# Folding the Newton step of the mLSTM head finish, and reordering the work around it and around the output projection that follows

## What is computed

```python
def _head_norm(x, g):
    xc = x - jnp.mean(x, axis=-1, keepdims=True)
    y = xc * lax.rsqrt(jnp.mean(xc * xc, axis=-1, keepdims=True) + NORM_EPS)
    return y.reshape(x.shape[:2] + (-1,)) * g
...
        hc = num / jnp.maximum(jnp.abs(den), jnp.exp(-m_t))[..., None]
...
    out_d = jax.nn.sigmoid(o_pre) * _head_norm(hm, P['mlstm_gn_g'][j])
    y = jnp.concatenate([out_c, out_d], axis=-1) @ P['c_w_out'][j]
    ...
        x = x + g1 * y
```

## Time and profile before

| | us |
|---|---|
| median of 3 runs (1537.2 to 1539.61) | 1537.5 |
| the profiled execution's own time | 1538.78 |
| its span, first to last instruction | 1537.2 |
| TensorE matmul busy in the span (93%) | 1428.2 |
| VectorE busy (58%) | 892.0 |
| ScalarE busy (33%) | 508.9 |
| GpSimd busy (8%) | 127.5 |

### The profile page before, as it was taken

One profiled execution on the slowest core, in us unless ns is written; L12 is line 12 of the kernel. 1 busy time (PEld: TensorE's weight loads), 2 busy tenths in 40 slices (PEclk: granted clock), 3 DMA queues, 4 the chain that ended last, 5 costly groups with the idle time before them and its releaser, 6 DMA issues.

```text
span 1537.2 us, 28543 instructions
## 1 busy us (share of the span) xinstructions
PE 1428.2 (93%) x11003; PEld 1353.7 (88%) x11003; DVE 892.0 (58%) x1613; ACT 508.9 (33%) x755; POOL 127.5 (8%) x149
## 2 busy tenths in 40 slices
PE   6899999969999999999679999987799999999997
PEld 4789898869999999999669897876699999999997
DVE  4565675578876885587764556664553433333344
ACT  4254345232222221222443334533332212222233
POOL 0000000002211220021000000000001101100100
PEclk9899999989999999999879899988899999999999
DMA  9443343325554554353222213221213223232222
GB/s 327 155 131 117 124 145 113 125 68 170 173 152 138 165 165 137 97 169 101 49 57 56 67 32 91 78 61 32 82 55 93 85 86 87 88 95 83 82 75 80
DMA packets 231853, 164.67 MB, mean 107 GB/s; under 512 B 9990, under 2 KB 218568, under 8 KB 231636
## 3 DMA queue, kind: packets, MB, share of 16 engines
q1 hardware_dynamic: 219716, 120.57, 26.8%
q0 software_dynamic: 11744, 42.75, 8.3%
q10 hardware_dynamic: 304, 0.10, 0.0%
HBM read 159.80 MB, written 3.60 MB: 106 GB/s over the span
## 4 chain that ended last, share of the span: by engine, by line
PE 75%; DVE 11%; ACT 7%; issue 4%; DMA 2%; SPq 0%; DVEq 0%; ACTq 0%; POOLq 0%
PE ring L604 67%; ACT weight_high L415 1%; DVE weight_low L420 1%; PE core_j L532 1%; DMA weight_raw<-in_c_w_in 1%; PE core_k L1317 1%; PE ring L2147 1%; PE ring L2229 1%; PE core_j L482 1%; DVE norm_rstd L614 1%; DVE norm_step L612 1%; PE core_k L1320 0%; DVE norm_step L611 0%; DVE normed_low L700 0%; DVE residual L710 0%
## 5 line engine op out<-in xcount | busy, mean ns | idle before, releaser
L604 PE MATMUL ring<-normed_high,weight_high 128*128 128x272 f32 x2128 | 454.7, 295 | 38.0 <-DVE normed_low L700 24.9
L604 PE MATMUL ring<-normed_high,weight_low 128*128 128x272 f32 x2128 | 446.2, 292 | 0.0
L604 PE MATMUL ring<-normed_low,weight_high 128*128 128x272 f32 x2128 | 445.4, 291 | 0.0
L604 PEld LDWEIGHTS ring<-normed_high,weight_high 128*128 128x128 f32 x2128 | 340.6, 192 | 49.0 <-issue 39.9
L604 PEld LDWEIGHTS ring<-normed_low,weight_high 128*128 128x128 f32 x2128 | 341.0, 192 | 0.0
L604 PEld LDWEIGHTS ring<-normed_high,weight_low 128*128 128x128 f32 x2128 | 338.9, 192 | 0.0
L420 DVE TENSOR_TENSOR weight_low<-weight_raw,weight_high 128x1024 fp32r<-128x1024 f32 x197 | 257.5, 1308 | 71.1 <-ACT weight_high L415 69.6
L415 ACT ACTIVATE weight_high<-weight_raw 128x1024 fp32r<-128x1024 f32 x197 | 206.8, 1050 | 164.7 <-PE ring L604 152.3
L604 PE MATMUL ring<-mixed_high,weight_high 128*128 128x272 f32 x960 | 203.6, 294 | 18.3 <-DVE weight_low L420 7.7
L604 PE MATMUL ring<-mixed_high,weight_low 128*128 128x272 f32 x960 | 200.7, 291 | 0.0
L604 PE MATMUL ring<-mixed_low,weight_high 128*128 128x272 f32 x960 | 199.9, 290 | 0.0
(11 more groups left out here) (403 smaller groups left out, 1166.9 us busy)
## 6 DMA issues: line engine op xcount, KB each, us to landing
weight_raw<-in_w_ffn_in SPq DMA_DIRECT2D x88, 512.0 KB, 3.7
mod_weight<-in_w_mod POOLq DMA_DIRECT2D x48, 512.0 KB, 4.2
mod_weight<-in_w_mod POOLq DMA_DIRECT2D x16, 1024.0 KB, 5.5
weight_raw<-in_w_ffn_out SPq DMA_DIRECT2D x32, 512.0 KB, 3.7
weight_raw<-in_a_w_in SPq DMA_DIRECT2D x24, 512.0 KB, 3.9
weight_raw<-in_c_w_in SPq DMA_DIRECT2D x20, 512.0 KB, 3.9
mixer_area<-in_w_mod SPq DMA_DIRECT2D x8, 1024.0 KB, 8.8
weight_raw<-in_w_ffn_out SPq DMA_DIRECT2D x16, 384.0 KB, 3.2
```

What stands on the lines that cost most here:

```text
L604: last = pe.matmul(PS[p.slot][:, half, 0:HALF], w[n.slot][:, k, :], x[:, k, half * HALF:(half + 1) * HALF], start=(k == 0 and w is WH and ...
```

## The change

The finish of the mLSTM heads is rewritten. With the centred values c, the first guess y of the reciprocal root and the variance v, it computes c (1 + gate) y (y y v - 3), with the gain changed from 0.5 to -0.25, instead of 0.5 c (1 + gate) times a separately refined y. The product c (1 + gate) is made early on VectorE, y y on ScalarE. The copies of the head out of PSUM go from ScalarE to VectorE. ScalarE's table load goes ahead of the weight copy in the loop. VectorE does the attention ahead of the low part of the head before. For the last head the squared floors are summed with the variance by matmuls, and Ln and the product read the sum from PSUM. The last k-tile of the first two output units is issued for both units with the high parts first. At the start of both output projections ScalarE makes the third unit's high weights ahead of the first square; in layer 1 VectorE makes its low weights ahead of the first sum.

```diff
...
         s_fth = sem("ffn_tanh")
+        s_hsq = sem("head_rstd_squared")
         s_area, s_smw, s_wg = sem("area_cleared"), sem("small_weights_in"), sem("decay_weights_in")
...
                 for j in range(2):
-                    if not (end and j) and not (first and j == 0):
+                    if first and j == 0:
+                        hi_of(act, Turn(w, 2))
+                    elif not (end and j) and not first:
                         hi_of(act, Turn(w, j + 1, 2, i))
...
                 for j in range(size):
-                    if not (end and j == size - 1) and not (first and j == 0):
+                    if not (end and j == size - 1) and not first:
                         lo_of(dve, Turn(w, j + 1, size, i))
                     residual_dve(dve, Turn(w, j, size, i), Turn(p, j, size, i), gate, i * size + j)
+                    if first and j == 0:
+                        lo_of(dve, Turn(w, 2))
                     if q is not None:
...
                     pe.wait_ge(s_glo, KD + (k + 1 if k >= HEADS else HEADS))
-                    last = product(pe, n, p, k, KD, (GH, GL))
-                if k == KD - 1:
-                    last.then_inc(s_used, 1)
+                    product(pe, n, p, k, KD, (GH, GL))
...
                 head_var(pe, OSQ, s_osq, h + 2 * HEADS)
+
+            def last_var():
+
+                pe.wait_ge(s_d2, HEADS)
+                pe.matmul(K[:, 0, :], MEAN[:, :], DD[:, 0:TP], start=True, stop=False)
+                pe.matmul(K[:, 1, 0:TS], MEAN[:, :], DD[:, TP:T], start=True, stop=False)
+                pe.wait_ge(s_osq, 3 * HEADS)
+                pe.matmul(K[:, 0, :], MEAN[:, :], OSQ[:, 0:TP], start=False, stop=True)
+                pe.matmul(K[:, 1, 0:TS], MEAN[:, :], OSQ[:, TP:T], start=False, stop=True).then_inc(s_var, 1)
+
+            def last_tile():
+
+                turns = [(Turn(W_OUT1, j), Turn(R_OUT1, j)) for j in range(2)]
+                k = KD - 1
+                pe.wait_ge(s_gah, 2 * KD + DONE0)
+                for n, p in turns:
+                    for w in (WH, WL):
+                        for half in range(2):
+                            pe.matmul(PS[p.slot][:, half, 0:HALF], w[n.slot][:, k, :],
+                                      GH[:, k, half * HALF:(half + 1) * HALF], start=False, stop=False)
+                pe.wait_ge(s_glo, 2 * KD)
+                for n, p in turns:
+                    for half in range(2):
+                        last = pe.matmul(PS[p.slot][:, half, 0:HALF], WH[n.slot][:, k, :],
+                                         GL[:, k, half * HALF:(half + 1) * HALF], start=False, stop=True)
+                    last.then_inc(s_used, 1)
...
             out1(1, range(4, 6))
-            var_of(HEADS - 1)
+            last_var()
             out1(1, range(6, 7))
-            out1(0, range(7, 8))
-            out1(1, range(7, 8))
+            last_tile()
...
-            def head_copies(h):
-                copy_head(act, st, s_nd, h + 2 * HEADS, h + 1)
+            def floors(h):
+                act.wait_ge(s_nd, h + 1)
                 act.wait_ge(s_nv, h + 2 * HEADS)
...
             def rstd(h):
-                act.preload_act_table_set("natural_log_exp_and_others")
-                act.wait_ge(s_nv, h + 2 * HEADS + 1)
-                st.done(act.activation(NR[:, :], NV[:, :], ACT.Ln))
+                if h < HEADS - 1:
+                    act.wait_ge(s_nv, h + 2 * HEADS + 1)
+                    st.done(act.activation(NR[:, :], NV[:, :], ACT.Ln))
+                else:
+                    act.wait_ge(s_var, 3 * HEADS)
+                    st.add(act.activation(NR[:, 0:TP], K[:, 0, :], ACT.Ln))
+                    st.done(act.activation(NR[:, TP:T], K[:, 1, 0:TS], ACT.Ln))
                 act.activation(NR[:, :], NR[:, :], ACT.Exp, scale=-0.5).then_inc(s_hr0, 1)
+                act.wait_ge(s_hr0, h + 2 * HEADS + 1)
+                act.activation(NT[:, :], NR[:, :], ACT.Square).then_inc(s_hsq, 1)
...
                 if h:
-                    head_copies(h - 1)
+                    floors(h - 1)
                 else:
...
                 values(h)
+                if h:
+                    act.preload_act_table_set("natural_log_exp_and_others")
                 hi_of(act, Turn(W_ML, 2 * h + 3))
...
                     gate(h + 1)
-            head_copies(HEADS - 1)
+            floors(HEADS - 1)
             squares(HEADS - 1)
+            act.preload_act_table_set("natural_log_exp_and_others")
             rstd(HEADS - 1)
...
             def floors(h):
+                dve.wait_ge(s_nd, h + 1)
+                st.add(dve.tensor_copy(OT[:, 0:TP], K[:, 0, :]))
+                dve.tensor_copy(OT[:, TP:T], K[:, 1, P:P + TS]).then_inc(s_o, 1)
                 dve.wait_ge(s_dabs, h + 1)
...
+            def gated(h):
+
+                dve.wait_ge(s_oc, h + 2 * HEADS + 1)
+                dve.wait_ge(s_dabs, h + 1)
+                st.add(dve.scalar_tensor_tensor(out=OB, in0=GATES[h % 2], scalar=1.0, in1=OC, op0=ALU.add,
+                                                op1=ALU.mult))
+
             def finish(h):
                 dve.wait_ge(s_var, h + 2 * HEADS + 1)
-                dve.wait_ge(s_d2, h + 1)
-                st.add(dve.tensor_tensor(NV[:, 0:TP], K[:, 0, :], DD[:, 0:TP], ALU.add))
-                dve.tensor_tensor(NV[:, TP:T], K[:, 1, 0:TS], DD[:, TP:T], ALU.add).then_inc(s_nv, 1)
-                dve.wait_ge(s_nv, h + 2 * HEADS + 1)
                 if h < HEADS - 1:
+                    dve.wait_ge(s_d2, h + 1)
+                    st.add(dve.tensor_tensor(NV[:, 0:TP], K[:, 0, :], DD[:, 0:TP], ALU.add))
+                    dve.tensor_tensor(NV[:, TP:T], K[:, 1, 0:TS], DD[:, TP:T], ALU.add).then_inc(s_nv, 1)
+                    dve.wait_ge(s_nv, h + 2 * HEADS + 1)
                     lo_of(dve, Turn(W_ML, 2 * h + 5))
                 dve.wait_ge(s_hr0, h + 2 * HEADS + 1)
-                newton(dve, st, NV[:, :], NR[:, :], NT[:, :])
-                st.done(dve.tensor_tensor(NT[:, :], OC, NR[:, :], ALU.mult))
-                dve.scalar_tensor_tensor(out=OB, in0=GATES[h % 2], scalar=1.0, in1=NT[:, :], op0=ALU.add,
+                st.wait()
+                st.add(dve.tensor_tensor(OB, OB, NR[:, :], ALU.mult))
+                dve.wait_ge(s_hsq, h + 1)
+                if h < HEADS - 1:
+                    st.done(dve.tensor_tensor(NT[:, :], NT[:, :], NV[:, :], ALU.mult))
+                else:
+                    st.add(dve.tensor_tensor(NT[:, 0:TP], NT[:, 0:TP], K[:, 0, :], ALU.mult))
+                    st.done(dve.tensor_tensor(NT[:, TP:T], NT[:, TP:T], K[:, 1, 0:TS], ALU.mult))
+                dve.scalar_tensor_tensor(out=OB, in0=NT[:, :], scalar=-3.0, in1=OB, op0=ALU.add,
                                          op1=ALU.mult).then_inc(s_ob, 1)
+
+            def low(h):
+                dve.wait_ge(s_ob, h + 2 * HEADS + 1)
                 dve.wait_ge(s_gah, h + KD + HEADS + DONE0 + 1)
...
                 norm_column(h)
+                if h:
+                    gated(h - 1)
                 keys(h)
...
                 attention(h)
+                if h:
+                    low(h - 1)
                 if h < HEADS - 1:
...
             floors(HEADS - 1)
+            gated(HEADS - 1)
             finish(HEADS - 1)
+            low(HEADS - 1)
...
             st.add(dve.tensor_scalar(HGAIN[:, 4:8], cols2("gla_gn_g", 4), 0.5, None, ALU.mult))
-            st.add(dve.tensor_scalar(HGAIN[:, 8:12], cols2("mlstm_gn_g", 4), 0.5, None, ALU.mult))
+            st.add(dve.tensor_scalar(HGAIN[:, 8:12], cols2("mlstm_gn_g", 4), -0.25, None, ALU.mult))
             dve.wait_ge(s_cth, 1)
...
```

## The result

The changed kernel took 1517.88 us (median, 1515.05 to 1520.58) beside 1538.55 us of the kernel before (1537.2 to 1543.31): a ratio of 0.9865, with a 95% interval of 0.9845 to 0.9885. The forecast of 1522.1 us was 4.2 us too long, and its lower end, 1518.5, lies 0.6 us above the median. Measured twice more, the same kernel gave 0.9854 (0.9837 to 0.9871) and 0.9905 (0.9878 to 0.9932), the last with a median of 1522.39 us. So the direction was right, the size was forecast a quarter too small (15.4 of 20.7 us), and the miss of 4.2 us is no larger than the distance between two measurements of the same kernel (1517.7 and 1522.39 us).

What follows compares the result with a forecast made beforehand. TensorE's work plus stalls on ScalarE and VectorE chains was taken as the bound; layer 0 0.2 + heads 2.1 + 3.3 + 6.4 + tail 3.4 = 15.4 us, so 1537.5 - 15.4 = 1522.1 us, range 1519.5 to 1524.5.

Steps and rivals of the forecast that it cites:

- What bounds the kernel, heads 1 to 3: Before the state update's second half, TensorE waits 2.12, 1.81 and 3.80 us for the preceding head's finish; all go.
- The clock in heads 2 and 3: Matmuls behind the removed stalls return to full clock: 1.31 and 0.21 us in head 2, 2.05 and 0.53 in head 3.
- Other work that moves: In the heads, PSUM copies, gated product, Square wait and low part cost TensorE nothing; Square's wait priced 0 to 0.1 us.
- The rival in which the low part becomes the wait: In the heads, the low part delays VectorE's states and the outputs wait; half of 11.8 us lost, 1528 us, chance 0.13.
- The tail and the third unit: Behind the last head, the last tile begins 2.5 us earlier and layer 1's third output unit 3.4 us earlier.
- Its second piece: In the last tile, unit 0 completes after five pairs of matmuls in place of three, 1.74 + 0.97 us, at 1056.7.
- Layer 0: At layer 0's third output unit, VectorE no longer stands 0.22 us for ScalarE's weight copy; gain 0.2 us.
- The sum, "it moves up whole": Projection and feed-forward after the third unit, set by TensorE, keep their length, so the whole 15.4 us reaches the end.

Runs made afterwards that it cites:

- all_again: The whole change measured once more, against the kernel before: 1517.7 us, ratio 0.9854.
- whole_2: The unchanged code of the changed kernel measured again, beside three other kernels on one chip: 1522.39 us, ratio 0.9905 to the kernel before.
- heads_only: Changed kernel with only the edits of heads 1 to 3 kept; tail, third units and layer 0 as before: 1526.47 us, ratio 0.9919.
- tail_only: Changed kernel with the finish in heads 1 to 3 as before; tail, third units and layer 0 as changed: 1532.0 us, ratio 0.9961.
- fill_before: Kernel before, with matmuls whose results are overwritten put into TensorE's waits of heads 1 to 3: 1534.99 us, ratio 0.9979.
- layer0_alone: Kernel before, with only layer 0's third-unit weight copy moved ahead of the square: 1539.73 us, ratio 1.0003.
- fill_tail: Changed kernel, with overwritten matmuls in TensorE's waits before the last tile and before the third unit: 1518.62 us, ratio 0.9862.
- var_on_vector: Changed kernel, with the last head's variance summed on VectorE as before: 1520.96 us, ratio 0.9878.

## Why the prediction was right or wrong

*What bounds the kernel, heads 1 to 3:* right. The three waits went, and the heads gained 12.0 us, forecast 11.8, in every execution that has their edits alone or with the tail's:

```
                to head 0   heads   tail   third unit to end   span
before            941.6     101.2   19.9        474.5         1537.2
changed           939.4      89.2   15.1        472.3         1516.0
all_again         939.3      89.2   14.9        474.2         1517.7
whole_2           940.7      89.2   15.9        474.4         1520.3
heads_only        941.4      89.2   19.7        474.8         1525.1
tail_only         938.8      99.2   16.2        472.9         1527.0
```

The finish leaves more room than it needs: in head 1 the attention stands idle for the scores, not for the finish. VectorE's timeline of the changed kernel:

```profile
961.73 0.73 DVE L2044 SCALAR_TENSOR_TENSOR mixer_area<-norm_step,mixer_area 128x544 f32<-128x544 f32 x1
965.16 0.69 DVE L1987 TENSOR_TENSOR mixer_area<-core_j,mixer_area 128x512 f32<-128x512 f32 x1 [2.70 <-PE core_j L1404]
```

The finish is done at 962.46, the attention starts at 965.16. The outputs of head 3 wait 0.35 us for the states, which I had set against a gain and taken as nothing.

*The clock in heads 2 and 3:* right in mechanism, 3.6 us by `fill_before` against 4.1.

*Other work that moves:* right; no copy, no gated product and no wait for Square shows up as a wait of TensorE. The rival in which the low part becomes the wait is out: the low part runs at 0.77 us between the query product and the states and TensorE waits for neither beyond those 0.35.

*The tail and the third unit:* the order of events was right and the size too small. The term was 3.4 us; the three executions of the whole change gained 4.8, 5.0 and 4.0. Its second piece was mis-sized: the last tile was costed at the low clock, 1.74 + 0.97 = 2.71 us for five pairs; in the first execution it took 1.31 + 0.47 = 1.78, in `whole_2` 2.18 + 0.47 = 2.65. I had named this, as up to 2.5 us less, in the forecast's own range only, not in the number. The rest is small: Ln begins 2.12 us behind the start of the sum both before and after, where I had 0.28 lost, and from Ln to the last tile the forecast of 4.6 us met 4.47, so the last tile starts 2.9 us earlier, forecast 2.5.

*Layer 0:* costed at 0.2 us; by `layer0_alone` it can't be told from nothing, with an interval of some 3 us to either side.

*The sum, "it moves up whole":* this is the step that failed. Of the 5.8 us by which the profiled gain of 21.2 exceeds the forecast's 15.4, the tail is 1.4 and the heads 0.2; 2.2 lie behind the third unit and 2.0 ahead of the heads, where nothing was to change but layer 0's 0.2. Behind the third unit it took 474.5 us before, and 472.3, 474.2 and 474.4 in the three executions of the changed kernel; the way to head 0 took 941.6 before and 939.4, 939.3 and 940.7. So two executions gained 2 us ahead of the heads and one of them 2 more behind. There the low clock differs: from 600 to 930 us the granted clock is 0.93 before and 0.94 in these two, and at the end of the kernel the windows of the first execution and of `all_again`, with the same number of matmuls in each, are

```profile
1400.00:1516.00 116.00, 103.69 (x818) 101.37 (x817) 50.09 (x72) 38.78 (x52) 8.19 (x6) 0.98 0.25 79
1400.00:1517.00 117.00, 107.93 (x818) 105.38 (x816) 49.98 (x72) 38.78 (x52) 8.19 (x6) 0.95 0.25 78
```

The prediction's clock had only the stretches behind the waits that it removed, and gave no range to those elsewhere, though the low clock takes 59 us of the kernel before, all but some 10 of them outside the marks (0.92 granted over the 121.1 us between), and the loss differs by several us from one measurement of the changed kernel to the next. Its lower end should have stood some 3 us lower. Against the third measurement, 1522.39, the forecast would have been 0.3 us off; that agreement is as much chance as the miss.

*Left open:* whether a part of the smaller loss in the first two measurements belongs to the change. Seven of eleven profiled executions with layer 0's edit reach head 0 before 939.5 us, and none of the six without it does (941.0 to 944.9), which speaks for some 2 us; the times of the four kernels on one chip show no such gain, with intervals that would hide it. The two measurements that are set side by side here, `all_again` and `whole_2`, were also taken on different chips, on which the kernel before differs by 0.9 us; the changed kernel is not known to have run twice on one chip, so what belongs to the chip stays open too.

## What to carry to other kernels

Take a step off the chain in front of TensorE's stall and check what is late next: that sum held here to 0.2 us in 12. When a kernel has low-clock stretches all along, price an edit's clock only where its own wait stood, and widen the range by what the stretches elsewhere change between executions. And measure small variants side by side on one chip: against a number from another occasion, an edit worth 0.4 us looked like 6.

## What was not expected of the hardware

Keeping TensorE busy through a wait kept its clock at 1.00 (`fill_before` in head 2, `fill_tail` in the tail), but the whole gained only 0.2% from it in the first case, and in the second the worth stays open, since no changed kernel was measured beside it. A wait of 1.3 us in head 0 was followed by 48 matmuls at 7.75 us in `var_on_vector`, while waits of 0.6 to 1.1 us at the same place in the other kernels were followed by 6.2; but the wait of 2.12 us in head 1 of the kernel before was followed by 6.21, so the length of the wait does not decide by itself. And two measurements of one kernel, 1517.7 and 1522.39 us, lie further apart than the runs of the kernel before beside them, 1538.93 and 1538.04.
